# Up projection by seven products: order of ScalarE's and VectorE's steps, place of the early splits, and PSUM banks of the chains

## The reference

```python
h2 = _rmsnorm(x, g_ffn)
f = jnp.einsum("btd,df->btf", h2, w_up)
f_gate, f_up = jnp.split(f, [D_FF], axis=-1)
f_conv, new_f = _causal_dwconv(f_gate, buf_f, conv_f_w)      # 3 taps
x = x + jnp.einsum("btf,fd->btd", jax.nn.silu(f_conv) * f_up, w_down)
```

## Time and profile before

| what | value |
|---|---|
| median of 3 runs | 849.6 us (849.23 to 850.08) |
| the profiled execution | 849.24 us, its span 847.1 us |
| TensorE (PE) busy | 835.9 us, 99% of the span |
| VectorE (DVE) busy | 678.1 us, 80% |
| ScalarE (ACT) busy | 413.9 us, 49% |
| up projection, from P1 of pair 1 to the down projection's first matmul | 490.39 to 712.81 us |

### The profile page before, as it was taken

One profiled execution on the slowest core, in us unless ns is written; L12 is line 12 of the kernel. 1 busy time (PEld: TensorE's weight loads), 2 busy tenths in 40 slices (PEclk: granted clock), 3 DMA queues, 4 the chain that ended last, 5 costly groups with the idle time before them and its releaser, 6 DMA issues.

```text
span 847.1 us, 18325 instructions
## 1 busy us (share of the span) xinstructions
PE 835.9 (99%) x6912; PEld 832.4 (98%) x6912; DVE 678.1 (80%) x1010; ACT 413.9 (49%) x748; POOL 128.9 (15%) x98
## 2 busy tenths in 40 slices
PE   8999999999999999999999999999999999999996
PEld 8999999999999999999999989999999999999996
DVE  5899998999999966766579899998998998644343
ACT  7753636464342235664236575564554657332232
POOL 2283838466000000000003200000000000000000
PEclk9999999999999999999999999999999999999999
DMA  9424233432333233227723113344323424453423
GB/s 261 126 82 118 76 99 91 140 105 81 111 103 100 85 108 92 78 73 133 190 77 99 46 55 101 100 115 110 92 84 101 132 72 138 109 134 100 100 70 114
DMA packets 189160, 88.92 MB, mean 105 GB/s; under 512 B 34758, under 2 KB 187644, under 8 KB 189076
## 3 DMA queue, kind: packets, MB, share of 16 engines
q1 hardware_dynamic: 186225, 86.29, 36.5%
q10 hardware_dynamic: 2875, 1.82, 0.8%
HBM read 83.79 MB, written 3.51 MB: 103 GB/s over the span
## 4 chain that ended last, share of the span: by engine, by line
PE 94%; DVE 4%; ACT 1%; issue 1%; ACTq 0%; DVEq 0%
PE psum L1842 44%; PE psum L1848 22%; PE psum L2018 12%; PE psum L2023 6%; PE psum L2046 4%; PE psum L2051 2%; PE psum L2167 1%; DVE w_lo L1434 1%; PE psum L2176 1%; PE psum L1885 1%; PE psum L1820 1%; PE psum L1883 0%; PE psum L1892 0%; DVE w_lo L1447 0%; DVE u L1595 0%
## 5 line engine op out<-in xcount | busy, mean ns | idle before, releaser
L1842 PE MATMUL psum<-act,w_hi 128*128 128x260 f32 x2600 | 341.1, 282 | 0.0
L1842 PEld LDWEIGHTS psum<-act,w_hi 128*128 128x128 f32 x2600 | 323.0, 188 | 0.0
L1139 DVE TENSOR_TENSOR w_lo<-raw,w_hi 128x1024 fp32r<-128x1024 f32 (+2 forms) x110 | 129.9, 1184 | 75.6 <-ACT w_hi L572 75.3
L1848 PE MATMUL psum<-act,w_lo 128*128 128x260 f32 x1300 | 185.1, 282 | 0.0
L1848 PEld LDWEIGHTS psum<-act,w_lo 128*128 128x128 f32 x1300 | 168.1, 188 | 0.0
L572 ACT ACTIVATE w_hi<-raw 128x1024 fp32r<-128x1024 f32 (+2 forms) x110 | 107.0, 976 | 86.0 <-PE psum L1848 83.4
L540 POOL TENSOR_TENSOR gate_a<-gate_a,prods 128x512 f32<-128x512 f32 x72 | 110.1, 1529 | 79.6 <-ACT prods L657 71.2
L2018 PE MATMUL psum<-act,w_hi 128*128 128x260 f32 x544 | 87.5, 285 | 2.3 <-ACT tmp L915 2.3
L2018 PEld LDWEIGHTS psum<-act,w_hi 128*128 128x128 f32 x544 | 75.5, 191 | 2.7 <-ACT tmp L915 2.7
L1216 DVE SCALAR_TENSOR_TENSOR psum<-u,cst,psum 128x512 f32<-128x512 f32 x96 | 66.8, 747 | 0.0
L1842 PE MATMUL psum<-mid,w_hi 128*128 128x260 f32 x512 | 66.5, 282 | 0.0
(11 more groups left out here) (208 smaller groups left out, 1016.8 us busy)
## 6 DMA issues: line engine op xcount, KB each, us to landing
raw<-in_w_in SPq DMA_DIRECT2D x56, 512.0 KB, 3.7
raw<-in_w_up SPq DMA_DIRECT2D x44, 512.0 KB, 3.9
raw<-in_w_down SPq DMA_DIRECT2D x16, 384.0 KB, 4.0
raw<-in_w_down SPq DMA_DIRECT2D x16, 320.0 KB, 3.2
v<-in_x_prompt SPq DMA_DIRECT2D x8, 512.0 KB, 6.6
raw<-in_w_b_out SPq DMA_DIRECT2D x8, 512.0 KB, 3.7
raw<-in_w_a_out SPq DMA_DIRECT2D x8, 512.0 KB, 5.3
raw<-in_w_o SPq DMA_DIRECT2D x8, 512.0 KB, 4.1
```

The source lines that it names most:

```text
L1139: ve.tensor_tensor(w_lo[:, slot, 0:k, :], raw[:, s, 0:k, :], w_hi[:, slot, 0:k, :], ALU.subtract).then_inc(lo_done, 1)
L1842: pe.matmul(a[:, h, :], w_hi[:, s, j, :], rhs(k, part)[:, h * H:(h + 1) * H], start=start and part == 0, stop=False)
L1848: last = pe.matmul(a[:, h, :], w_lo[:, s, j, :], rhs(k, 0)[:, h * H:(h + 1) * H], start=False, stop=stop)
```

## The change

Nothing is added to or taken from TensorE's work; its matmuls stand in the same order. What changes:

- In pair 0, `hi_open` stands ahead of `hi_2`, `root_eps` directly behind `weight_sum_1`, and `weight_sum_4` behind the reciprocal.
- `up_1` of pair 1 goes directly behind the dummy Silu, ahead of `hi_4` and `hi_3`.
- The five early splits, one each in pairs 1 to 5, go into plain pairs: two in pair 5, two in pair 10, one in pair 15.
- The orders of four kinds of pairs are written anew, on both engines (`step_at_end_of_run` loses only its early split).
- Some chains use other PSUM banks, and the last gate too. Two waits are written differently: `weight_sum_1` now waits until `lo_2` of the last seven-product pair has read the sums, and `up_22` waits for the product of the last seven-product pair instead of that of pair n-1.

The constants first, then ScalarE's functions, then VectorE's (`BANK_X`, the tables `hi_step` and `lo_step` that count the splits, VectorE's `step_in_run` and the last lines of the stage are left out):

```diff
-    EARLY_HI = 5
+    EARLY = {5: (0, 1), 10: (2, 3), 15: (4,)}
+    EARLY_HI = sum(len(t) for t in EARLY.values())
...
-        BANK_GATE = {0: 0, 5: 1, 10: 2, 15: 0, 21: 1}
+        BANK_GATE = {0: 0, 5: 1, 10: 2, 15: 0, 21: 2}
...
             def step_of_first(n):
+                hi_open(n + 1)
                 hi_2(n + 1)
-                hi_open(n + 1)
                 sc.wait_ge(var_eps, 2)
                 sc.activation(x_root_row, rinv, ACT.Sqrt).then_inc(var_root, 1)
                 sc.activation(rs, ms, ACT.Silu).then_inc(table_set, 1)
+                up_1(n + 1)
             def step_of_plain(n):
                 conv_first(n - 1)
+                hi_up(n)
                 hi_2(n + 1)
-                hi_up(n)
+                hi_open(n + 1)
                 silu(n - 1)
+                for i in EARLY.get(n, ()):
+                    up_hi(i)
+
+            def step_of_second(n):
+
+                up_v(n)
+                hi_3(n)
                 hi_open(n + 1)
-                if n <= EARLY_HI:
-                    up_hi(n - 1)
-
-            def step_of_second(n):
+                conv_first(n - 1)
+                hi_4(n)
+                up_5(n)
+                hi_2(n + 1)
+                silu(n - 1)
+
+            def step_behind_plain(n):
                 hi_4(n)
                 hi_3(n)
                 up_1(n)
                 conv_first(n - 1)
+                up_v(n)
+                hi_open(n + 1)
+                silu(n - 1)
+                up_5(n)
+                hi_2(n + 1)
+
+            def step_in_run(n):
+
+                hi_4(n)
+                up_1(n)
+                conv_first(n - 1)
+                hi_3(n)
                 hi_open(n + 1)
                 up_v(n)
                 silu(n - 1)
                 up_5(n)
-                if n <= EARLY_HI:
-                    up_hi(n - 1)
-                hi_2(n + 1)
-
-            def step_behind_plain(n):
-
-                hi_3(n)
-                conv_first(n - 1)
-                up_1(n)
-                hi_4(n)
-                up_v(n)
-                hi_open(n + 1)
-                up_5(n)
-                silu(n - 1)
-                if n <= EARLY_HI:
-                    up_hi(n - 1)
-                hi_2(n + 1)
-
-            def step_in_run(n):
-
-                hi_4(n)
-                conv_first(n - 1)
-                up_1(n)
-                hi_3(n)
-                hi_open(n + 1)
-                silu(n - 1)
-                up_v(n)
-                up_5(n)
-                if n <= EARLY_HI:
-                    up_hi(n - 1)
                 hi_2(n + 1)
             def step_at_end_of_run(n):
...
                 gate, up = raw_at(n, "gate"), raw_at(n, "up")
                 ve.wait_ge(raw_in[gate], raw_up(n))
                 ve.wait_ge(raw_in[up], raw_up(n))
+                if NTH[n] > 0:
+                    ve.wait_ge(q_lo, LO["2", LAST_SEVEN[n]])
                 if n == 1:
                     ve.wait_ge(mm_done, G_O + RING + 1)
                 ve.tensor_tensor(s1_s2[:, 0], raw_even(up), raw_odd(up), ALU.add).then_inc(w_sum, 1)
...
             def up_22(n):
                 ve.wait_ge(p_done, PRODUCT["P7", n])
                 ve.wait_ge(snap, 3 * NTH[n] + 3)
-                ve.wait_ge(prod_done, START + 2 * KT + n)
+                if NTH[n] > 0:
+                    ve.wait_ge(prod_done, START + 2 * KT + LAST_SEVEN[n] + 1)
                 ve.tensor_tensor(c22, bank_x(n), snap_5, ALU.add).then_inc(c22_set, 1)
             def conv_in_free(n):
...
                 weight_sum_1(n + 1)
+                root_eps(2, square_banks, RMS_EPS)
                 weight_sum_2(n + 1)
+                lo_open(n + 1)
                 weight_sum_3(n + 1)
                 lo_2(n + 1)
-                lo_open(n + 1)
-                root_eps(2, square_banks, RMS_EPS)
-                weight_sum_4(n + 1)
                 ve.wait_ge(var_root, 2)
                 ve.reciprocal(rinv, x_root_row).then_inc(rinv_done, 1)
+                weight_sum_4(n + 1)
             def step_of_plain(n):
...
                 lo_up(n)
                 lo_2(n + 1)
+                lo_open(n + 1)
                 up_product(n - 1)
-                lo_open(n + 1)
                 weight_sum_4(n + 1)
-                if n <= EARLY_HI:
-                    up_lo(n - 1)
+                for i in EARLY.get(n, ()):
+                    up_lo(i)
                 if n == PLAIN[2]:
                     turn_root()
             def step_of_second(n):
-                lo_4(n)
                 weight_sum_1(n + 1)
                 ve.wait_ge(rinv_done, 2)
                 plain_gate(n - 1)
+                weight_sum_2(n + 1)
+                lo_3(n)
+                weight_sum_3(n + 1)
+                lo_open(n + 1)
+                lo_4(n)
+                conv_rest(n - 1)
+                weight_sum_4(n + 1)
+                up_22(n)
+                plain_product(n - 1)
+
+            def step_behind_plain(n):
+
+                plain_gate(n - 1)
+                weight_sum_1(n + 1)
                 lo_3(n)
                 weight_sum_2(n + 1)
-                conv_rest(n - 1)
-                lo_open(n + 1)
-                plain_product(n - 1)
-                weight_sum_3(n + 1)
-                up_22(n)
-                weight_sum_4(n + 1)
-                if n <= EARLY_HI:
-                    up_lo(n - 1)
-
-            def step_behind_plain(n):
-
-                plain_gate(n - 1)
-                weight_sum_1(n + 1)
-                weight_sum_2(n + 1)
-                lo_3(n)
                 conv_rest(n - 1)
                 weight_sum_3(n + 1)
                 lo_4(n)
                 lo_open(n + 1)
                 plain_product(n - 1)
+                weight_sum_4(n + 1)
                 up_22(n)
-                weight_sum_4(n + 1)
-                if n <= EARLY_HI:
-                    up_lo(n - 1)
             def step_in_run(n):
```

More of the change, by code:

```diff
@@ L310, in build @@
         assert PLAIN[0] == 0 and PLAIN[-1] == FT - 1 and SEVEN[1]
-        BANK_X = {1: 3, 2: 1, 3: 2, 4: 0, 6: 0, 7: 3, 8: 0, 9: 1, 11: 1, 12: 2, 13: 1, 14: 3, 16: 3, 17: 1, 18: 3, 19:
-                  2, 20: 0}
-        BANK_GATE = {0: 0, 5: 1, 10: 2, 15: 0, 21: 1}
+        BANK_X = {1: 3, 2: 1, 3: 2, 4: 0, 6: 3, 7: 0, 8: 1, 9: 0, 11: 1, 12: 3, 13: 0, 14: 2, 16: 3, 17: 1, 18: 2, 19:
+                  0, 20: 1}
+        BANK_GATE = {0: 0, 5: 1, 10: 2, 15: 0, 21: 2}
         assert len(BANK_X) + len(BANK_GATE) == FT
@@ L350, in hi_step @@
             if n in (0, FT - 1):
-                return (("up", n), ("2", n + 1), (opening(n + 1), n + 1)) if n == 0 else (("up", n),)
+                return (("up", n), (opening(n + 1), n + 1), ("2", n + 1)) if n == 0 else (("up", n),)
             if not SEVEN[n]:
-                return (("2", n + 1), ("up", n), (opening(n + 1), n + 1))
+                return (("up", n), ("2", n + 1), (opening(n + 1), n + 1))
             if not FOLLOWS[n]:
-                return (("4", n), ("3", n), (opening(n + 1), n + 1), ("2", n + 1)) if n == 1 else \
-                    (("3", n), ("4", n), (opening(n + 1), n + 1), ("2", n + 1))
+                return (("3", n), (opening(n + 1), n + 1), ("4", n), ("2", n + 1)) if n == 1 else \
+                    (("4", n), ("3", n), (opening(n + 1), n + 1), ("2", n + 1))
             return (("4", n), ("3", n), (opening(n + 1), n + 1), ("2", n + 1)) if SEVEN[n + 1] else (("3", n), ("4", n), (opening(n + 1), n + 1))
@@ L365, in lo_step @@
             if not FOLLOWS[n]:
-                return (("4", n), ("3", n), (opening(n + 1), n + 1)) if n == 1 else \
+                return (("3", n), (opening(n + 1), n + 1), ("4", n)) if n == 1 else \
                     (("3", n), ("4", n), (opening(n + 1), n + 1))
@@ L1033, in _ @@
                     step_at_end_of_run(n)
-            hi_up(FT - 1)
             conv_first(FT - 2)
@@ L1038, in _ @@
             silu(FT - 2)
+            hi_up(FT - 1)
             down_hi(0, PRODUCT["P5", FT - 2])
@@ L1690, in _ @@
             up_gate(FT - 2)
+            conv_rest(FT - 2)
             lo_up(FT - 1)
-            conv_rest(FT - 2)
             up_product(FT - 2)
```

1 line of the change is left out of this document (removed).

## The result

| | before | changed kernel |
|---|---|---|
| median of 7 runs | 849.6 us (849.2 to 850.08) | 846.82 us (846.62 to 846.98) |
| ratio, 95% interval | | 0.9966 (0.9956 to 0.9976) |
| span of the profiled execution | 847.1 us | 845.0 us |
| down projection's first matmul | 712.81 us | 710.62 us |

The account below looks back on a forecast made before the run. The prediction took TensorE, busy 99% of the span, as the bound, so only its pauses could be won back: 1.90 + 0.27 + 0.25 = 2.42 us off the profiled 849.24 gave 846.8 us, range 845.6 to 848.4.

Parts of the forecast that it names:

- The bound and the second limit in pair 1: TensorE bounds; in pair 1, behind P6's 2.06 us wait for `up_1`, P3 waits for `up_5`, Silu, convolution and reciprocal.
- The working through pair 1: Step-by-step start times in pair 1 with the change: five waits of 2.20 us in all replace 4.10 us.
- Gain 1.90 us: Pair 1: the new order lets pair 2's P4 start at 502.63 instead of 504.52.
- Pair 3, pair 5 and the splits: 0.27 and 0.25: Pair 3 wins 0.27 us from `up_1` ahead of `conv_first`, early splits leaving; pair 5 wins 0.25 from `hi_up` ahead of `hi_2`.
- Cover of the splits in plain pairs: Pairs 5, 10 and 15: VectorE's slack covers the added splits of 0.61, 1.22 and 0.61 us.
- The table rule: Pair 1's table switches: a further gap behind each load shrinks the gain by 1.3 us, time 848.1; chance 2 in 100.
- Rival 1, the clock: Pair 1: the clock falls again, 3.2 us at half clock, loss taken at 1.1, time 847.9; chance 0.18.
- Rivals 2 and 3: 2: later pairs give the gain back, 848.6, chance 0.10. 3: VectorE late in seven-product runs, 851.6, chance 0.05.
- Rival 4: Pair 1: half of the 2.2 us of waits left does not appear, time 845.7; chance 0.08.

Follow-up runs that it names:

- the copy alone: Kernel before with one instruction moved: `up_1` of pair 1 directly behind the dummy Silu; 849.53 us against 849.5.
- third sums on GpSimd: Changed kernel with the third weight sum of pairs 2, 3 and 4 on GpSimd instead of VectorE; 848.02 us, kernel before 849.34.
- copy and epsilon: Kernel before with `up_1` of pair 1 directly behind the dummy Silu and `root_eps` directly behind the first sum; 849.56 us against 849.34.

## Why the prediction came out right, and where it was right for the wrong reason

*The bound and the second limit in pair 1.* Right, and shown: with the copy alone P6 starts 1.5 us earlier and P3 no earlier, because P3's start hangs on reciprocal, convolution, Silu and `up_5`.

*The working through pair 1.* Right to about 0.1 us. Taking the 0.29 off: P6 493.26 (forecast 493.26), `lo_3`'s end 497.80 (497.83), P3 498.84 (498.90), pair 2's P1 501.02 (500.95), P4 502.59 (502.63).

*"Gain 1.90 us" for pair 1.* As a local figure right, P4 of pair 1 starts 1.94 us earlier than 504.53. As a term of the sum it holds only with the rest of the change: undoing it costs 1.7 (1.9 by the starts), having it alone wins 0.0.

*Pair 3, pair 5 and the splits: 0.27 and 0.25.* The sum was right and its division wrong, in two ways. By place, the table of starts gives 1.84 up to P6 of pair 2, 0.58 from there to P6 of pair 4, 0.31 to P6 of pair 6, and 0.25 lost again behind it, most of it in pair 11: 2.48, where 1.90 + 0.27 + 0.25 = 2.42 was forecast. Pair 3 was read too small, by TensorE's idle time instead of by starts as in pair 1, and the loss in pair 11 was put at nothing; that the two errors cancel is luck. By part of the change, the prediction gave the early splits almost nothing of their own ("leave pairs 1 to 4", a help to the 0.27 of pair 3), but putting them back costs 2.2 us, and moving them alone wins all 0.9 of pairs 3 and 5 (by starts) without any new order. `hi_up` ahead of `hi_2` got 0.25, but undoing it costs 0.2 or nothing. The step that failed is the adding up of the parts' terms as if they were independent. VectorE is the second bound from pair 0 to pair 4: 28.99 of 30 us busy between 504 and 534 even in the changed kernel (97%; between 586 and 638 it is 94%).

```profile
504.00:534.00 30.00, 30.00 (x252) 30.00 (x252) 28.99 (x43) 16.82 (x33) 0.00 (x0) 1.00 0.41 115
...
586.00:638.00 52.00, 52.00 (x434) 51.88 (x433) 49.11 (x77) 29.48 (x54) 0.00 (x0) 1.00 0.36 102
```

That VectorE sets the pace there is also what the starts say: the four kernels with the early splits in pairs 1 to 5 reach P4 of pair 1 anywhere from 12.25 to 15.17 us behind P1, and P6 of pair 6 all between 59.44 and 59.83. There, time that pair 1 wins is only kept if VectorE has as much less to do behind it; the place of the copies decides 0.5 us. By medians, pair 1 alone wins 0.0, the splits alone 0.0, pair 1 with all new orders but the early splits in place 0.5, the splits with all new orders but the old pairs 0 and 1 1.0, all but the order in runs 2.0, and all together 2.8.

*Cover of the splits in plain pairs.* The prediction said that it is VectorE's slack. Alone, the splits made a pause of 0.98 us in pair 11; with the new order behind plain pairs 0.15 to 0.25 us is lost there.

*The table rule.* No gap stood behind the loads again: the load at 489.24 took 1.28 and the root began at 490.53. The drain that the Trainium skill, "ScalarE: Activation LUTs", section "What ACT_TABLE_LOAD costs", adds to each switch does not show in this kernel.

*Rival 1, the clock.* It did not fall in the changed kernel's up projection, where the longest break between matmuls was 0.5 us. What the experiments add is that its fall is not certain after a pause of 2.06 us (once at half clock, in the kernel before; twice not, with pairs 0 and 1 as before and with the splits moved alone), that it cost nothing in the kernel before, and that it cost 1.0 us on the spot with the copy moved alone, near the 1.1 of the prediction. *Rivals 2 and 3*: no marked pause came in the runs behind pairs 5, 10 and 15; the short delays of pair 11 are rival 2's mechanism in one pair of twelve. *Rival 4*: the waits left in pair 1 are real, 2.2 us by starts of matmuls, and 2.2 was forecast.

Open: the new PSUM banks and `step_behind_plain` were not taken out by themselves in any run. The gains of pair 1 and of pairs 3 and 5 appear with the old banks too (pairs 0 and 1 changed alone, splits moved alone), so neither needs the new ones. Open also are the 0.3 us between the 2.48 of the starts and the 2.8 of the medians, and the up to 0.3 us by which single executions differ ahead of the up projection.

## What to carry to other kernels

When TensorE's waits are short and in one place, look for the engine that is full around them, and ask of each gain by reordering who else is late there: a wait that is removed comes back at the next semaphore unless that engine's work goes too. Measure the parts alone and the whole without each part; here two parts (pairs 0 and 1; the splits) that each win nothing alone win 2.8 us together with the new orders, 2.0 of it without the order in runs. Measure what a pause costs by the starts of the work around it, not by the marked idle time. Put copies that an engine awaits ahead of instructions that wait for the full engine.

## What the runs showed of the hardware that was not expected

- GpSimd holds VectorE up: VectorE's 128x512 sum of two SBUF operands took 1.39 us beside GpSimd's 1.30 us sum, and 0.68 us otherwise. The Trainium skill, "GPSIMD Engine Reference", section "Specifications", says that GpSimd shares its SBUF interfaces with VectorE and lists VectorE's instructions with two SBUF inputs among those that contend; the trace agrees.
- The same pause of TensorE, 2.06 us, was followed by 3.2 us at 1.2 GHz in one profiled execution and by none in two others of the same work in pair 1. Pauses of 2.41 and 2.60 us (copy moved alone, copy and epsilon) were followed by half clock; pauses of 1.24 and 1.43 us (third sums on GpSimd, pairs 0 and 1 changed alone) and all shorter ones in the up projection were not.
